# Rotary positions of two mixers from a second, half-swapped copy of the rows instead of a product with a rotation table

## The reference

```
def apply_rope(x, cos, sin):
    x1, x2 = jnp.split(x, 2, axis=-1)
    rot = jnp.concatenate([-x2, x1], axis=-1)
    return (x * cos[None, :, None, :] + rot * sin[None, :, None, :]).astype(x.dtype)
```

## Time and profile before

| | |
|---|---|
| median of 3 runs | 4452.1 us (4442.47 to 4460.52) |
| the profiled execution, whole | 4446.81 us |
| its span, first to last instruction | 4445.0 us |
| mean granted TensorE clock | 0.879 of full speed |
| busy: PE / DVE / ACT / POOL | 80% / 52% / 31% / 13% of the span |
| PE MATMUL records | 17648 |

### The profile page before, as it was taken

One profiled execution on the slowest core, in us unless ns is written; L12 is line 12 of the kernel. 1 busy time (PEld: TensorE's weight loads), 2 busy tenths in 40 slices (PEclk: granted clock), 3 DMA queues, 4 the chain that ended last, 5 costly groups with the idle time before them and its releaser, 6 DMA issues. The chain is left out here.

```text
span 4445.0 us, 48347 instructions
## 1 busy us (share of the span) xinstructions
PE 3571.7 (80%) x17648; PEld 2945.2 (66%) x17648; DVE 2295.1 (52%) x4294; ACT 1363.8 (31%) x2522; POOL 576.9 (13%) x450
## 2 busy tenths in 40 slices
PE   7857888578779998775498898879997774688887
PEld 6646776467568887554377776658886564476776
DVE  3366533665347875556563232367865655553232
ACT  2213322133233332333323131233333333324131
POOL 0001000010003432000102010023321001002010
PEclk9957899578889999887699999989998986799999
DMA  4331143311242323221152222432223221343322
GB/s 137 111 90 44 39 112 109 92 44 39 78 123 85 99 67 99 81 67 50 52 156 81 81 76 76 122 115 86 76 69 95 81 75 30 101 119 85 84 76 76
DMA packets 566928, 375.21 MB, mean 84 GB/s; under 512 B 73988, under 2 KB 497924, under 8 KB 566428
## 3 DMA queue, kind: packets, MB, share of 16 engines
q1 hardware_dynamic: 566684, 372.01, 29.4%
HBM read 313.94 MB, written 58.00 MB: 84 GB/s over the span
## 5 line engine op out<-in xcount | busy, mean ns | idle before, releaser
L817 PE MATMUL bank<-h,w_hi 128*128 128x512 f32 (+1 forms) x1264 | 568.5, 450 | 72.2 <-DVE w_low L860 55.2
L819 PE MATMUL bank<-h,w_low 128*128 128x512 f32 (+1 forms) x1264 | 516.6, 409 | 0.0
L818 PE MATMUL bank<-h,w_hi 128*128 128x512 f32 (+1 forms) x1264 | 516.5, 409 | 0.0
L455 DVE TENSOR_TENSOR w_low<-w,w_hi 128x1024 fp32r<-128x1024 f32 (+1 forms) x170 | 257.8, 1517 | 399.6 <-ACT w_hi L449 398.9
L449 ACT CAST w_hi<-w 128x1024 fp32r<-128x1024 f32 (+1 forms) x170 | 204.2, 1201 | 599.2 <-DMA w<-in_w_mlp 338.5
L817 PEld LDWEIGHTS bank<-h,w_hi 128*128 128x128 f32 (+1 forms) x1264 | 252.9, 200 | 141.4 <-DVE w_low L860 64.0
L573 PE MATMUL bank<-h,w_hi 128*128 128x512 f32 (+1 forms) x720 | 290.7, 404 | 42.8 <-DVE w_low L455 42.8
L818 PEld LDWEIGHTS bank<-h,w_hi 128*128 128x128 f32 (+1 forms) x1264 | 252.7, 200 | 57.4 <-issue 13.6
L819 PEld LDWEIGHTS bank<-h,w_low 128*128 128x128 f32 (+1 forms) x1264 | 249.8, 198 | 59.6
L574 PE MATMUL bank<-h,w_hi 128*128 128x512 f32 (+1 forms) x720 | 287.4, 399 | 0.0
L575 PE MATMUL bank<-h,w_low 128*128 128x512 f32 (+1 forms) x720 | 287.3, 399 | 0.0
(11 more groups left out here) (427 smaller groups left out, 7450.1 us busy)
## 6 DMA issues: line engine op xcount, KB each, us to landing
w<-in_w_in SPq DMA_DIRECT2D x148, 512.0 KB, 4.1
z<-z_tile SPq DMA_DIRECT2D x212, 256.0 KB, 2.3
w<-in_w_gate SPq DMA_DIRECT2D x64, 512.0 KB, 4.1
w<-in_w_mlp SPq DMA_DIRECT2D x64, 512.0 KB, 4.1
w<-in_w_mlp SPq DMA_DIRECT2D x32, 1024.0 KB, 5.6
q_twice<-z SPq DMA_DIRECT2D x128, 128.0 KB, 2.8
w<-in_w_out SPq DMA_DIRECT2D x32, 512.0 KB, 4.0
w<-in_w_branch SPq DMA_DIRECT2D x64, 256.0 KB, 3.0
```

Of the source, the lines that this page charges most:

```text
L455: self.v.tensor_tensor(self.wl[s][:, :, 0:n], self.w[s][:, :, 0:n], self.wh[s][:, :, 0:n].bitcast(F32), ALU.subtract).then_inc(self.w_low. ...
L817: self.t.matmul(bank[0:n, :], wh, self.k.hH[:, j, :], start=j == 0, stop=False)
L818: self.t.matmul(bank[0:n, :], wh, self.k.hL[:, j, :], start=False, stop=False)
L819: m = self.t.matmul(bank[0:n, :], wl, self.k.hH[:, j, :], start=False, stop=j == KD - 1)
```

## The change

Diff and Swa use a new class, `SwappedRotation`. The rotation table `rot2` goes; the sign goes into the sin table. For every item SP issues, after the two ordinary row loads, four more DMAs (`swap_sp`) of 32 rows each that write the same 64 rows of z, halves exchanged, into the item's `rope_tmp` tile. Before these, SP waits until the item that used this `rope_tmp` tile before (4 items back in Diff, 2 in Swa) has been added. PE has no rotation matmul any more, but its steps and shares of the stream stay. POOL multiplies x by cos as soon as the row loads have landed. DVE multiplies `rope_tmp` by sin in place, after the swapped rows have landed, and goes on as before. In Diff and Swa the SP generator now yields after each item, so an item's loads stand behind the stream's pieces of the step before, and the values' loads come after the last item.

```
-    def rotate_pe: self.t.matmul(bank, rot, x)
+class SwappedRotation(Rotation):
+    def swap_sp(self, p, i, src):
+        n, half = p * self.items + i, HD // 2
+        if n >= self.ring:
+            self.s.wait_ge(*self.roped.nth(n - self.ring))
+        for at in range(0, P, HD):
+            for a, b in ((0, half), (half, 0)):
+                self.s.dma_start(self.rtmp[n % self.ring][at + a:at + a + half, :],
+                                 src[b:b + half, :]).then_inc(self.swapped_in[n % self.ring].sem, 16)
+    def rotate_pe(self, p):
+        for _ in range(self.items + 2):
+            yield self.share
+    def rotate_pool(self, p):
...
+            self.p.wait_ge(*self.row_in(p, i))
+            self.p.tensor_tensor(x, x, cos, ALU.mult).then_inc(self.cosined.sem, 1)
...
+    def rotate_dve(self, p):
...
+                tmp = self.rtmp[n % self.ring][:, :]
+                self.v.wait_ge(*self.swapped_in[n % self.ring](n // self.ring))
+                self.v.tensor_tensor(tmp, tmp, sin, ALU.mult).then_inc(self.sined.sem, 1)
...
@@ Diff.sp and Swa.sp
                 for out, src in twice(self.place(i)[0], z[at:at + HD, :]):
                     s.dma_start(out, src).then_inc(self.rows_in[i].sem, 16)
+                self.swap_sp(p, i, z[at:at + HD, :])
+                yield
...
-            for _ in range(self.items + 3):
+            for _ in range(3):
                 yield
```

More of the change, by code:

```diff
@@ L53 @@
           "nsa": ("cos1", "sin1", "rot1", "cosc", "sinc", "cmpneg", "cmpone"),
-          "rope": ("cos2", "sin2", "rot2", "lam"),
+          "rope": ("cos2", "sin2", "lam"),
           "gdn": ("levlow", "levup", "sup", "slow", "carryf", "carryb")}
@@ L97, in constants @@
     out["cosc"], out["sinc"], _ = rope(500000.0, 16, ends)
-    out["cos2"], out["sin2"], out["rot2"] = rope(10000.0, 64, np.arange(T))
+    out["cos2"], out["sin2"], _ = rope(10000.0, 64, np.arange(T))
+    out["sin2"] = np.where(i % HD < HD // 2, -out["sin2"], out["sin2"])
     tq = np.arange(NT)[None, :, None] * P + np.arange(P)[:, None, None]
@@ L1839, in rotate_dve, with init_rotation @@
             yield
+class SwappedRotation(Rotation):
+    def init_rotation(self, items, ring, tables):
+        super().init_rotation(items, ring, tables)
+        self.swapped_in = [self.sig(f"swapped_in{r}", -(-2 * items // ring), by=64) for r in range(ring)]
+    def swap_sp(self, p, i, src):
[10 more added lines that the diff above has]
+    def rotate_pool(self, p):
+        cos = self.k.tab(self.rope_tables[1])
+        for i in range(self.items):
+            x = self.place(i)[0][:, :]
+            self.p.wait_ge(*self.row_in(p, i))
+            self.p.tensor_tensor(x, x, cos, ALU.mult).then_inc(self.cosined.sem, 1)
+            yield
+        yield
+        yield
+    def rotate_dve(self, p):
+        sin = self.k.tab(self.rope_tables[2])
+        for i in range(self.items + 2):
+            if i < self.items:
+                n = p * self.items + i
+                tmp = self.rtmp[n % self.ring][:, :]
+                self.v.wait_ge(*self.swapped_in[n % self.ring](n // self.ring))
+                self.v.tensor_tensor(tmp, tmp, sin, ALU.mult).then_inc(self.sined.sem, 1)
+            if 0 <= i - 1 < self.items:
+                n, x = p * self.items + i - 1, self.place(i - 1)[0][:, :]
+                self.v.wait_ge(*self.sined(p, i - 1))
+                self.v.wait_ge(*self.cosined(p, i - 1))
+                self.v.tensor_tensor(x, x, self.rtmp[n % self.ring][:, :], ALU.add).then_inc(self.roped.sem, 1)
+            if i >= 2:
+                x, low, high, scale = self.place(i - 2)
+                self.v.wait_ge(*self.high(p, i - 2))
+                if scale is None:
+                    self.v.tensor_tensor(low[:, :], x[:, :], high[:, :].bitcast(F32), ALU.subtract).then_inc(self.made.sem, 1)
+                else:
+                    self.v.scalar_tensor_tensor(high[HD:P, :], x[HD:P, :], scale, high[HD:P, :].bitcast(F32),
+                                                ALU.mult, ALU.subtract).then_inc(self.made.sem, 1)
+            yield
@@ L2921, in rows_dve @@
             self.v.tensor_copy(self.k.yT[:, self.first + 2 * p + j, :], self.row_banks[j][:, :]).then_inc(self.y_stored.sem, 1)
-class Diff(Attention, Rotation, NormedHeads):
+class Diff(Attention, SwappedRotation, NormedHeads):
     maps, mixes = 2, True
@@ L2940, in __init__ @@
         self.init_attention(8)
-        self.init_rotation(8, 4, ("rot2", "cos2", "sin2"))
+        self.init_rotation(8, 4, ("", "cos2", "sin2"))
         self.init_heads(8, 4, self.bank[4:6])
@@ L3074, in pool @@
             yield
-class Swa(Attention, Rotation, NormedHeads):
+class Swa(Attention, SwappedRotation, NormedHeads):
     sinks = True
@@ L3090, in __init__ @@
         self.init_attention(16)
-        self.init_rotation(5, 2, ("rot2", "cos2", "sin2"))
+        self.init_rotation(5, 2, ("", "cos2", "sin2"))
         self.first, self.row_banks = 8, self.bank[4:6]
```

## The result

The changed kernel takes 4495.4 us (median of 4), the kernel before 4447.3 us (median of 4, the three shown and one run beside it): ratio 1.0101, interval 1.0069 to 1.0134, 48 us slower. The profiled execution of after took 4484.4 us, the lowest of its four; that of before 4446.8 us, at its median. The two profiles are thus 37.6 us apart.

What follows compares the result with a forecast made beforehand. DVE's chain of product with sin, sum, high and low part was taken to end the stretches, PE waiting. Diff's 5.0 + 4.3 and Swa's 8.1 + 11.7 us make 29.1 a layer, 58 in two: 4452.1 to 4510 us, range 4460 to 4555.

Steps and rivals of the forecast that it cites:

- The price of an issue: SP's queue: a 32-row load takes 0.50 us, range 0.33 to 0.64, so an item costs 3.3 us instead of 1.27.
- The rivals of cheap and of dear issues: SP's loads: at 0.33 us about 4463 us, chance 0.15; at 0.64 or more with lower PE clock 4558, chance 0.12.
- Diff, forecast 38.7 us: Diff's stretches, first row load to last low part: 38.7 us, 5.0 and 4.3 more than before; bounds 30 and 45.
- the hold at a store: SP's queue in Diff: a store waiting for ACT's tanh holds later loads 1.9 us once a tile, 4.6 us in all.
- The tail: Diff, after the last issue: landing 2.8, product and sum 1.2, high part 0.6, low part 0.7, signals 0.2, together 5.5 us.
- Swa, forecast 30.3 us: Swa's stretches, first row load to last low part: 30.3 us, 8.1 and 11.7 more than before; bounds 25.1 and about 36.
- The serial ring: Swa's ring of 2: an item's swapped loads wait for the sum two items back, making a cycle of 6.1 us.
- the landing: Swa's cycle: 2.8 us for swapped rows to land, added after four issues taking 2.0 us.
- PE's 45 us: PE's 52 rotation products, 0.86 us each: none of 45 us gained; rival that PE sets the pace, 4407 us, chance 0.05.
- The ports: DVE's product with sin loses its immunity beside POOL; rival that DVE and POOL taking turns decide: 4483 us, chance 0.08.
- the last sign: Before each attention PE should wait 5 us or more for q_stacked; without growth of that wait, the forecast mechanism is wrong.
- The clock: PE idles more and its matmuls come at half clock: 0 booked in the sum, 4 to 16 us at the upper end.

Runs made afterwards that it cites:

- ahead: Changed kernel with SP issuing as many items' loads as the ring has tiles in its first step, then one item per step: 4482.2 us, ratio 1.0066.
- short_pool: Changed kernel with POOL's product with cos cut to 8 of 512 columns, all waits kept: 4486.5 us, ratio 1.0080.
- idle_loads: Kernel before plus the four 32-row loads per item into spare tiles nobody reads, with the yield after each item: 4501.0 us, ratio 1.0114.
- act_queue: Changed kernel with three swapped loads per item issued from ScalarE's queue, row loads in one burst in SP's queue: 4467.2 us, ratio 1.0033.

## Why the prediction was right, point by point

- Sign and place: right. The growth lies in the eight stretches, forecast 58 us, measured 44.6 us in the stretches of the profiles and 48 us between the medians. Of the 13.6 us between 58 and 44.6, Swa was forecast 16.7 us too long and Diff 2.9 us too short. The median of the kernel before also fell from 4452.1 to 4447.3 us with one more run.
- The price of an issue, taken at 0.50 us between bounds of 0.33 and 0.64: 0.50 measured in Diff, on average of four. The middle of two bounds was a guess, and that it came out is luck; one issue takes 0.31, 0.42 or 0.58 us according to its place (last section), and behind the ring's wait in Swa four take 1.70 us. The rivals of cheap and of dear issues fell with it.
- Diff, forecast 38.7 us: measured 40.3, 38.9, 38.7 and 39.9. Term by term in the first part, from 1741.64: the items' issues 25.8 (26.4 forecast), the stream's issues with the gaps 2.3 (2.2), the hold at a store 3.7 (4.6), last issue to last low part 8.4 (5.5). That the sum is so close is partly luck. The hold was forecast as 2.4 holds of 1.9 us; each of the four stretches has one, of 3.7, 2.1, 2.1 and 3.2 us, since the last store stands behind the last item. The tail was mis-sized by 2.4 to 3.0 us the other way. I had counted only the last item's own operations; DVE still had the item before, held by POOL, and the stream's weights in front:

```profile
1772.88 1.03 DVE L1882 TENSOR_TENSOR rope_tmp<-rope_tmp,rope_tables 128x512 f32<-128x512 f32 x1 [2.28 <-DMA rope_tmp<-z]
...
1773.84 1.78 DVE L1887 TENSOR_TENSOR q_twice<-q_twice,rope_tmp 128x512 f32<-128x512 f32 x1
...
1775.54 0.68 DVE L1892 TENSOR_TENSOR k_twice_low<-k_twice,k_hi 128x512 fp32r<-128x512 f32 x1
...
1776.14 1.21 DVE L861 TENSOR_TENSOR w_low<-w,w_hi 128x1024 fp32r<-128x1024 f32 x1
...
1777.27 0.68 DVE L1882 TENSOR_TENSOR rope_tmp<-rope_tmp,rope_tables 128x512 f32<-128x512 f32 x1
```

  The last item's rows had landed, for the last product carries no wait, but DVE came to it only at 1777.27. The coupling between a store and the rotation, worked out from the order of the queues alone, is what ahead took away.
- Swa, forecast 30.3 us: measured 26.2, 25.7, 26.6 and 25.9. The serial ring is there, but a cycle takes 4.5 us, not 6.1. The step that failed is the landing: 2.8 us is counted from the start of an issue, and I laid it behind the end of the issue, and took the row loads' value for smaller loads. From the end of the four issues to the product it is 1.47 us (2057.68 to 2059.15). The rest of the cycle is 1.70 for the issues (2.0 forecast) and 1.3 for product and sum (1.2). Three cycles of 1.6 us too much in four stretches are 19 us, more than the whole difference between 58 and 45 us.
- PE's 45 us, booked at 0: nearly. Put back into the changed kernel they cost 4 to 6 us, not clear of nothing, and cut by 33 us in the kernel before they gave 12. "Takes nothing off the end" holds from a part's second product on, where DVE hardly pauses. At the head of a part it fails: there DVE waited for PE's first banks, for 5.1 us in Diff's first part. The forecast lacked this gain.
- The ports: booked at 0; short_pool gives 9 us for taking POOL's work away altogether, within the spread. All 52 products with sin had lasted 693 ns at most; now they last up to 1771, and each of the 18 above 0.7 us ran beside a POOL product, as the one at 1772.88 in the lines above, which ended 0.5 us after POOL's (1772.11 to 1773.37). The cost was mostly covered. By the rule of the Trainium skill, page "SBUF — State Buffer", section "SBUF: two separate sides", the product, now with two SBUF inputs, had to lose its immunity. The trace agrees with these numbers.
- What I said PE would wait for was wrong, and by the letter of the last sign ("if PE's wait before the attention does not grow, its mechanism is wrong") the mechanism would fall. PE's wait for q_stacked was 0.65, 4.31 and 7.53 us; it is now none, 3.1 and 2.4 us. The sign was badly chosen. PE does idle more, it is busy for 22.10 of 40.3 us in Diff's first part where it was for 26.66 of 33.7, but its in-order queue meets other waits first: for the stream's w_low in Diff (15.9 us in the first part), for the values' load in Swa (6.5 and 20.7 us). The values were booked at nothing and cost nothing, since the last low part comes later than they.
- The clock: the mean went from 0.879 to 0.869, in Diff's stretches from 0.85 and 0.90 to 0.67 and 0.76. Hardly a cost of it can be told from the rest. In Diff's first part the matmuls behind a wait of 5.4 us came 0.43 us apart at a granted clock of 0.50 instead of 0.23 at 1.00, and PE reached the values 0.8 us after the last low part; as a whole the mixers grew by 22.1 and 23.4 us, the stretches by 22.3 in each layer.

## What to carry to other kernels

Ask of a removed operation which chain ends the stretch in which it stands; here an engine busy for 80% of the span was waiting there for another, but for the head of each part. Count a DMA also as an entry of an in-order queue: its issue time, the semaphores ahead of it in that queue, and what stands behind it. With a ring of buffers, count how many round trips of issue, landing and use can be open at once, and count the landing from where the profile counts it.

## What the runs showed of the hardware

- The time of a load's issue in SP's queue follows the load ahead of it more than its own size. In the changed kernel a load of 32 rows took 0.58 us behind one of 64 rows, 0.42 us behind one of 32 rows and 0.31 us after a wait of SP; a load of 64 rows took 0.60 us behind one of 64 rows and 0.45 us behind one of 32. So three loads (32, 64 and 32 rows) took 1.76 us, 0.58, 0.51 and 0.58 with the gaps, nearly as long as four of 32 rows (1.97 us). Why is open. In ScalarE's queue the median was 0.55 us. Single issues of the changed kernel, of which the timelines above show the sums:

```profile
1757.25 0.58 SPq L1858 DMA_DIRECT2D rope_tmp<-z  x1
...
1757.88 0.42 SPq L1858 DMA_DIRECT2D rope_tmp<-z  x1
...
1763.33 0.45 SPq L3047 DMA_DIRECT2D q_twice<-z  x1
...
1763.82 0.60 SPq L3047 DMA_DIRECT2D q_twice<-z  x1
...
2055.98 0.31 SPq L1858 DMA_DIRECT2D rope_tmp<-z  x1
```

- Loads that nobody reads (idle_loads) cost as much as the whole change, while the same bytes from another queue (act_queue) left Diff's stretches within 2 us of what they were, at a higher DMA rate (230 GB/s in the first part, against 188 GB/s in the changed kernel).
